# Program's end of a transformer block: norm weights load into two ring rows, finished tiles are stored in the last phase, the last group's splits go first, VectorE norms two tiles

## The reference, cut to what matters

```python
def peer_ffn(x, wq, k1, k2, u, v):
    ...
    def expert_block(args):
        xb, eb, gb = args
        h = jnp.einsum('td,ted->te', xb, u[eb])
        a = jax.nn.gelu(h, approximate=False) * gb
        return jnp.einsum('te,ted->td', a, v[eb])
...
ffn = peer_ffn(h, peer_wq[l], peer_k1[l], peer_k2[l], peer_u[l], peer_v[l])
h = layer_norm(DEEPNORM_ALPHA * h + ffn, ln2_g[l], ln2_b[l])   # (x - mean) * rstd * g + b, over 1024 features
```

## Time and profile before

| what | value |
|---|---|
| median of 3 runs | 3171.38 us (3163.99 to 3172.98) |
| the profiled execution, its own time | 3172.34 us |
| its span, first to last instruction | 3170.7 us |
| VectorE busy, whole span | 2329.7 us (73%) |
| TensorE busy, whole span | 2656.3 us (84%) |
| GpSimd busy, whole span | 1602.5 us (51%) |
| mean granted TensorE clock | 0.925 of full speed |

### The profile page before, as it was taken

How to read it: one execution, slowest core, us unless ns; L and a number is a source line. 1 busy time by engine, 2 the same in 40 slices (tenths; PEclk the granted TensorE clock), 3 DMA queues, 4 the chain that set the end, 5 groups by cost and what they waited for, 6 DMA issues and landing times.

```text
span 3170.7 us, 40717 instructions
## 1 busy us (share of the span) xinstructions
PE 2656.3 (84%) x14888; PEld 2069.8 (65%) x14888; DVE 2329.7 (73%) x4931; ACT 1052.5 (33%) x1647; POOL 1602.5 (51%) x1190
## 2 busy tenths in 40 slices
PE   7997688889996565654667999999999999998886
PEld 6886577777775455642445767676767666776775
DVE  4511566665999799974767778777777887779999
ACT  4311333332554577751112222322222222222222
POOL 0001001112887455536666665766665776756674
PEclk9988799999998788876888999999999999999998
DMA  4222312222111599989999999999999999998994
GB/s 136 93 87 76 129 43 84 84 81 85 51 51 32 183 314 316 308 264 378 379 389 387 384 388 348 397 381 381 388 384 341 407 408 407 406 376 312 338 342 175
DMA packets 309791, 833.42 MB, mean 263 GB/s; under 512 B 26112, under 2 KB 114624, under 8 KB 309600
## 3 DMA queue, kind: packets, MB, share of 16 engines
q0 software_dynamic: 150864, 548.60, 45.3%
q1 hardware_dynamic: 158736, 282.31, 25.5%
HBM read 771.93 MB, written 58.88 MB: 262 GB/s over the span
## 4 chain that ended last, share of the span: by engine, by line
DVE 15%; DMA 13%; PE 10%; POOL 10%; issue 6%; ACT 0%; POOLq 0%; DVEq 0%
DMA e_u_row<-in_u,ids 12%; POOL hold L1904 7%; DVE e_u_row L2123 5%; POOL e_u_row L1895 3%; DVE e_y L2113 3%; PE psum L1965 2%; PE psum L1944 2%; PE psum L1946 1%; PE psum L1945 1%; DVE e_ul L2079 1%; PE psum L1966 1%; PE psum L1967 1%; DVE e_vl L2083 1%; DVE e_al L2100 1%; DVE hold L2132 1%
## 5 line engine op out<-in xcount | busy, mean ns | idle before, releaser
L2123 DVE CUSTOM_DVE_ANT_0 e_u_row<-e_u_row,hold 128x1024 f32<-128x1024 f32 x384 | 468.4, 1225 | 267.4 <-DMA e_u_row<-in_u,ids 248.4
L1895 POOL DMA_INDIRECT e_u_row<-in_u,ids x384 | 483.8, 1260 | 358.1 <-DVE ids L2123 235.3
L1965 PE MATMUL psum<-e_vh,e_ah 128*128 128x512 f32 x1024 | 429.4, 419 | 141.1 <-DVE e_y L2113 101.5
L1904 POOL DMA_INDIRECT hold<-in_v,ids x384 | 431.6, 1124 | 142.1 <-issue 113.0
L1966 PE MATMUL psum<-e_vl,e_ah 128*128 128x512 f32 x1024 | 416.4, 407 | 0.0
L1967 PE MATMUL psum<-e_vh,e_al 128*128 128x512 f32 x1024 | 413.7, 404 | 0.0
L1965 PEld LDWEIGHTS psum<-e_vh,e_ah 128*128 128x128 f32 x1024 | 202.1, 197 | 252.7 <-DVE e_y L2113 138.0
L1944 PE MATMUL psum<-x1d,e_uh 128*128 128x512 f32 x864 | 341.3, 395 | 0.0
L2113 DVE TENSOR_TENSOR e_y<-e_y,psum 128x512 f32<-128x512 f32 x504 | 324.2, 680 | 19.5 <-PE psum L1967 15.1
L1945 PE MATMUL psum<-x1d,e_uh 128*128 128x512 f32 x864 | 337.3, 390 | 0.0
L1946 PE MATMUL psum<-x1d,e_ul 128*128 128x512 f32 x864 | 336.3, 389 | 0.0
(11 more groups left out here) (399 smaller groups left out, 5663.4 us busy)
## 6 DMA issues: line engine op xcount, KB each, us to landing
e_vr<-in_v SPq DMA_DIRECT2D x128, 512.0 KB
e_ur<-in_uT SPq DMA_DIRECT2D x108, 512.0 KB
s_G<-g_tile SPq DMA_DIRECT2D x8, 4096.0 KB, 26.5
e_g<-s_G SPq DMA_DIRECT2D x64, 512.0 KB
ids<-in_w_ch SPq DMA_DIRECT2D x17, 512.0 KB, 4.0
s_ch<-p_out POOLq DMA_DIRECT2D x16, 512.0 KB
hold<-in_wq SPq DMA_DIRECT2D x16, 512.0 KB, 8.9
hold<-in_v,ids POOLq DMA_INDIRECT x476, 6.7
```

What stands on the lines that cost most here:

```text
L1895: pool.indirect_dma_start(out=u_ring[n % U_RING][:], out_offset=None, in_=io["u"], in_offset=bass.IndirectOffsetOnAxis(ap=id_u[:, s, k:k + ...
L1904: pool.indirect_dma_start(out=v_ring[m % V_RING], out_offset=None, in_=io["v"], in_offset=bass.IndirectOffsetOnAxis(ap=id_v[:, t:t + 1], a ...
L1965: nc.tensor.matmul(acc, ah[s][j][:, r], vh[s][j][:, c], start=(j == 0), stop=False)
L2123: nc.vector.tensor_tensor_reduce(row, row, xs[:, s, :], 1.0, 0.0, ALU.mult, ALU.add, hs[:, s, k:k + 1]).then_inc(dotted, 1)
```

## The change

Four parts. (1) The gain and bias are loaded by SP at group 54 into two rows of the ring, which shrinks from 11 to 9 rows. (2) Tiles 0 to 2 get their gain on DVE at the start of groups 56, 57 and 59 (`SCALED`), their bias on POOL after `gather_last(46)`, `(58)` and `(81)` (`SHIFTED`), and their store from SP at the start of groups 60, 61 and 63 (`SENT`). (3) The last group is written out apart, in another order: both v splits and both a splits earlier, the last row sums at its end. (4) Tiles 6 and 7 no longer take shift, ACT, gain and POOL's bias, but two DVE steps: (x - mean) x gain, and that x rstd + bias.

```diff
-        lng, lnb = (ur[j].rearrange("p k e -> p (k e)") for j in range(2))
-        ln_in = 16 * (NG + 1)
+        ln_in = [sem(f"f_ln_in{j}") for j in range(2)]
...
-        sum_ring = u_ring[1:] + v_ring
+        sum_ring = u_ring[1:] + v_ring[:V_RING - 2]
+        lng, lnb = v_ring[V_RING - 2:]
...
+        SCALED = tuple(PHASE[NS - 1] + n for n in (3, 4, 6))
+        SHIFTED = tuple((g + 1 - PHASE[NS - 1]) * P // (NG - PHASE[NS - 1]) for g in SCALED)
+        SENT = tuple(g + 4 for g in SCALED)
...
+                def send(t):
+                    if t < NT - 2:
+                        sp.wait_ge(done, t + 1)
+                    else:
+                        sp.wait_ge(done_last, t - NT + 3)
+                    sp.dma_start(out[0, t * P:(t + 1) * P, :], rows_of(t)).then_inc(stored, 16)
...
+                    if g == PHASE[NS - 1] + 1:
+                        sp.wait_ge(weighted, STEPS)
+                        for row, src, landed in zip((lng, lnb), ("ln2_g", "ln2_b"), ln_in):
+                            sp.dma_start(row, io[src].partition_broadcast(P)).then_inc(landed, 16)
+                    if g in SENT:
+                        send(SENT.index(g))
                     load_gates(g)
...
-                for j, src in enumerate(("ln2_g", "ln2_b")):
-                    sp.wait_ge(u_lo[j], NG - SHORT)
-                    sp.dma_start(ur[j].rearrange("p k e -> p (k e)"), io[src].partition_broadcast(P)).then_inc(u_in[j], 16)
-                for t in range(NT):
-                    sp.wait_ge(done, t + 1)
-                    sp.dma_start(out[0, t * P:(t + 1) * P, :], rows_of(t)).then_inc(stored, 16)
+                for t in range(NS - 1, NT):
+                    send(t)
...
+                def offset(t):
+                    if t == 0:
+                        pool.wait_ge(ln_in[1], 16)
+                    pool.wait_ge(nrm_g, t + 1)
+                    nc.gpsimd.tensor_tensor(rows_of(t), rows_of(t), lnb, ALU.add).then_inc(done, 1)
+
                 for n in range(P):
                     gather_last(n)
-                for t in range(NT):
-                    if t == 0:
-                        pool.wait_ge(u_in[1], ln_in)
-                    pool.wait_ge(nrm_g, t + 1)
-                    nc.gpsimd.tensor_tensor(rows_of(t), rows_of(t), lnb, ALU.add).then_inc(done, 1)
+                    if n in SHIFTED:
+                        offset(SHIFTED.index(n))
+                for t in range(NS - 1, NT - 2):
+                    offset(t)
...
                     if t + 1 < NT:
                         root_of(t + 1)
-                    normalize(t)
+                    if t < NT - 2:
+                        normalize(t)
...
+                def centre_last(t):
+                    dve.wait_ge(aggr, t + 1)
+                    nc.vector.scalar_tensor_tensor(rows_of(t), rows_of(t), mv[:, t, 0:1], lng,
+                                                   ALU.subtract, ALU.mult).then_inc(centred_last, 1)
+
+                def scale_last(t):
+                    dve.wait_ge(rooted, t + 1)
+                    nc.vector.reciprocal(rstd[:, t:t + 1], root[:, t:t + 1]).then_inc(inverted, 1)
+                    dve.wait_ge(inverted, t + 1)
+                    dve.wait_ge(centred_last, t - NT + 3)
+                    dve.wait_ge(ln_in[1], 16)
+                    nc.vector.scalar_tensor_tensor(rows_of(t), rows_of(t), rstd[:, t:t + 1], lnb,
+                                                   ALU.mult, ALU.add).then_inc(done_last, 1)
...
+                    if g in SCALED:
+                        weight(SCALED.index(g))
+                    if g == NG - 1:
+                        break
                     dot_rows(g, 0)
...
+                dot_rows(NG - 1, 0)
+                dot_rows(NG - 1, 1)
+                weigh(NG - 1, 0)
+                split_a(NG - 1, 0)
+                split_v(NG - 1, 0)
+                dot_rows(NG - 1, 2)
+                weigh(NG - 1, 1)
+                split_a(NG - 1, 1)
+                gather(NG - 2, 0, 2)
+                dot_rows(NG - 1, 3)
+                gather(NG - 2, 2, 4)
+                split_v(NG - 1, 1)
+                dot_rows(NG - 1, 4)
+                gather(NG - 2, 4, 6)
+                dot_rows(NG - 1, 5)
+                gather(NG - 2, 6, Q)
+                dot_rows(NG - 1, 6)
+                dot_rows(NG - 1, 7)
                 dve.wait_ge(summed, P)
...
-                for t in range(NS - 1):
-                    weight(t)
-                for t in range(NS - 1, NT + 2):
-                    if t < NT:
-                        if t >= NS:
-                            gather(NG - 1, 2 * (t - NS), 2 * (t - NS) + 2)
-                        statistics(t)
-                    if NS <= t <= NT:
+                for t in range(NS - 1, NT):
+                    if t >= NS:
+                        gather(NG - 1, 2 * (t - NS), 2 * (t - NS) + 2)
+                    statistics(t)
+                    if NS <= t < NT - 1:
                         shift_of(t - 1)
                     if t >= NS + 1:
                         weight(t - 2)
+                    if t == NT - 2:
+                        centre_last(t)
+                scale_last(NT - 2)
+                centre_last(NT - 1)
+                scale_last(NT - 1)
```

More of the change, by code:

```diff
@@ L1815, in experts @@
         v_landed = [sem(f"v_rows_landed{n}") for n in range(V_RING)]
-        s_landed = [sem(f"last_row_landed{n}") for n in range(U_RING - 1 + V_RING)]
+        s_landed = [sem(f"last_row_landed{n}") for n in range(U_RING - 3 + V_RING)]
         dotted = sem("u_row_dotted")
@@ L1822, in experts @@
         stored = sem("f_stored")
+        centred_last, done_last = sem("f_centred_last"), sem("f_done_last")
         stat, aggr, rooted, inverted, shifted, nrm, nrm_g, done = (
@@ L2163, in weight @@
                     dve.wait_ge(nrm, t + 1)
-                    dve.wait_ge(u_in[0], ln_in)
+                    dve.wait_ge(ln_in[0], 16)
                     nc.vector.tensor_tensor(rows_of(t), rows_of(t), lng, ALU.mult).then_inc(nrm_g, 1)
+                def centre_last(t):
[10 more added lines that the diff above has]
+                                                   ALU.mult, ALU.add).then_inc(done_last, 1)
                 nc.vector.memset(column[:], 0.0).then_inc(cleared, 1)
```

## The result

| what | before | after |
|---|---|---|
| median of 20 runs | 3169.37 us | 3180.04 us (3174.82 to 3190.49) |
| ratio after / before | | 1.0035, 95% interval 1.0026 to 1.0044 |
| the profiled execution, its own time | 3172.34 us | 3181.38 us |
| its span | 3170.7 us | 3179.7 us |

The change makes the kernel slower by 10.7 us by the medians, 0.35% by the ratio. The median lies inside the range that was given (3166 to 3182), but the forecast of no change, with 0.87, did not come in: the ratio of 1.0035 lies past the 0.3% bound on the slower side, which had 0.09, though its interval reaches down to 1.0026.

A forecast was written before the change was run, and what follows sets the result against it. The prediction took DVE to bound the last phase. Its terms, -6.0 + 3.4 + 2.55 + 3.7 = +3.65, say +3.7 us on 3171.4, gave a median of 3175 us, range 3166 to 3182, forecast as no change.

The forecast's parts named there:

- The bound: Group 54 to the end of the last group: DVE alone sets the pace, busy 233.85 of 234 us.
- The end behind S: From the last group's end on DVE to the last bias or DVE step: 31.13 us falls to 25.15, -6.0.
- The three gains: Gains of tiles 0 to 2, moved into groups 56, 57 and 59, cost DVE the same time there: +3.4 us.
- POOL's biases: Three biases in the loop: POOL waits until the PSUM additions, DVE loses 1.25 us each, +3.7; bounds 0 and 7.0.
- rival B: POOL gets in at the next boundary each time, DVE loses 2.34 us: +7.0 for the biases, 3178.5 us; chance 0.28.
- the place of 3092.30: Where DVE sums a slot 2 row and begins 7.67 us of instructions with two SBUF inputs; POOL's bias was expected then.
- SP: Loads at group 54, stores at 60, 61 and 63, ahead of the gates: cost nothing; 7.7 us if cover were gone.
- The last group's order: Last group: DVE idles 0.75, 1.1 and 0.7 us before the a splits and a v split, +2.55; bounds 1.5 and 2.6.
- The ring of nine: Ring of fetched rows shrinking from 11 to 9: nine steps give 19.7 us against a fetch's 9.0, so no cost.
- D: Rival: POOL gets in only at the third pair of additions, the ring runs dry: +13.6, 3185 us; chance 0.08.
- C: Rival: the costs in the loop don't come and the real saving of 2.6 us stays: 3169 us; chance 0.12.
- the likeliest case: Over the whole kernel, the sum of all terms, +3.65 us, giving 3175 us; chance 0.52.

The follow-up runs named there:

- late_stores: Changed kernel with the stores of tiles 0 to 2 moved back behind the last group; ratio to the kernel before 1.0025, last stretch 306.2 us.
- extras_behind: Changed kernel with the gain and bias loads and three stores issued behind the second v slab instead of ahead of the gates; ratio 1.0031, last stretch 302.7 us.
- old_last_group: Changed kernel with the old order of the last group; ratio to the kernel before 1.0035, last stretch 306.1 us.
- bias_with_psum: Changed kernel with POOL's biases of tiles 0 to 2 waiting to begin with DVE's additions from PSUM; ratio 1.0022, last stretch 304.1 us.
- two_norms_alone: Kernel before with only the two DVE steps for tiles 6 and 7 (part 4); ratio 0.9995, last stretch 293.0 us.
- three_norms: Kernel before with the two DVE steps for tiles 5, 6 and 7; ratio 1.0001, last stretch 292.0 us.
- gain_as_stt: Kernel before with the gains of tiles 1 and 2 done by scalar_tensor_tensor instead of tensor_tensor; single run, last stretch 295.6 us.
- new_order_alone: Kernel before with only the new order of the last group; ratio 1.0015, last stretch 300.9 us.
- new_order_ring_9: Kernel before with the new order of the last group and a ring of 9 rows instead of 11; ratio 1.0024, last stretch 300.7 us.
- bias_in_row_sums: Changed kernel with POOL's biases of tiles 0 to 2 asked for right behind the last v split of groups 56, 57 and 59; single run, last stretch 317.1 us.

## Why the prediction was off, point by point

**The bound.** Right. DVE sets the pace, and every part of the 12.7 us is a length or an idle time of DVE. (the earlier trace rows start at group 55, not 54; group 54 of the kernel before is the same, 26.14 us busy of 26.14.)

**The end behind S: -6.0.** Right, -6.3. The blocked `scale_last(6)` came as said: 3.50 us from 3169.62 to 3173.12 against 3.64.

**The three gains: +3.4.** Right.

**POOL's biases: +3.7.** This step failed: +6.5, near rival B's 7.0. The step took POOL to wait "until the additions from PSUM", by the row of the three gains in the kernel before, which was called the nearest. POOL got in at the next boundary every time: in groups 56, 57 and 59 of the changed kernel, late_stores, extras_behind and old_last_group, twelve instructions of 3.38 to 3.42 us. (The twelve are one course: POOL's start lies 0.22 to 0.26 us ahead of the boundary in each. In the changed kernel it came to the bias 2.8 to 3.9 us after DVE had reached the place of 3092.30 that the step names, not at it.) What the step took for its price, 1.25, is the price when the bias is made to start with the additions (bias_with_psum), so the size was right for a course that it didn't take. The Trainium skill ("SBUF — State Buffer", Who interferes with whom) has it that whoever issues first has the shared port for its whole instruction. The loop agrees with it: read to the letter it gave 7.0, and 6.5 were measured. Not every row of this case does: in the kernel before, two_norms_alone, three_norms and gain_as_stt POOL asked 0.9 us ahead of a boundary and had to let one more DVE instruction pass. With the new last group, same instructions and same distance, it got in. What decides there stays open.

**SP: 0.** This step failed: +4.0. It weighed 0.5 MB at the whole rate of the DMA engines (1.5 us at 340 GB/s) and against the fetches' slack. But the gates behind it have a slack of their own, 10.4 to 10.9 us, and a transfer of half a megabyte on this queue landed 6.3 to 9.7 us after issue by itself, and 11.0 to 12.4 with another right ahead. The bound given with the step, 7.7 in all if the cover were gone, would have held it. extras_behind shows the cause: with the same bytes behind the slabs, nothing waits for gates. The prediction had named this as its sign of being wrong (idle time on DVE in groups 54 to 62, gates late behind the new stores), and it came.

**The last group's order: +2.55.** The waits were the right ones, the size was not: +5.0. The two waits of 0.7 came as said. The middle one, for the slab's high part, was put at 1.1 with bounds that allowed no more; it is 0.9 to 1.7 in five kernels and 2.2 to 3.2 in three (the whole change, late_stores, bias_with_psum). By itself the order costs 3.1 to 3.3 us (new_order_alone, new_order_ring_9); the other 1.7 of the 5.0 are this wait. The slab took 7.7 us to land in the changed kernel, issued at 3123.43. The ring is not the reason, and the third store at most for a small part (new_order_ring_9 1.3, late_stores 2.7). The reason for the spread is not settled. That the new order is worth its 2.5 us by TensorE's earlier start was also too kind: 2.0 measured (30.75 - 28.78).

**The ring of nine: 0.** Right.

**Rivals.** B was right on its part. D did not come; bias_in_row_sums shows it with POOL held up for 13 us; in bias_with_psum 5.2 us of it did no harm. C did not come. Three terms were too small at once (biases by 2.8 us, SP by 4.0, the last group by 2.45), no single rival covered that, and the likeliest case came out 9 us short on a stretch of 300. That the median still fell into the range is in part luck: the three runs behind the forecast had a median of 3171.4 us, twenty have 3169.4, and the medians differ by 10.7 us where the last stretch of the profiled executions differs by 12.7. With 12.7 on 3171.4 it would have been 3184, outside.

## What to carry to other kernels

Moving work from a program's end into its last stage gains nothing when the same engine is full in that stage: the three gains cost 3.4 us in the loop and had cost 3.4 behind it. It gains only where an instruction or a wait disappears, as POOL's last bias does here. A transfer added to a queue must be weighed against the slack of what stands behind it in that same queue, and at that queue's own landing times, which the trace gives, not at the engines' whole rate. GpSimd's addition of 2.34 us on SBUF beside a full VectorE cost VectorE nearly the whole operation, 2.17 us; started together with additions that read PSUM, it cost 1.25.

## What the runs showed of the hardware that was not expected

- A VectorE instruction over 128 x 1024 elements on two SBUF inputs, in front of which GpSimd has got in, takes 3.36 to 3.42 us instead of 1.22 to 1.28, and counts as busy: groups 56 and 57 show 29.44 of 29.44 and 29.70 of 29.81 us busy while 2.17 us of each are lost.
- Who gets in at a boundary can differ between two kernels with the same instructions at the same distances: behind the last group POOL's first bias, asked for 0.9 us ahead, took 3.18 us with the new last group (the third gain 3.36) and 4.36 to 4.38 with the old one (the third gain 1.21 to 1.24).
- TensorE's granted clock was at half (0.50, the 1.2 GHz level) for a while in the changed kernel's last group: from 3137.88 on a matmul's step was 0.43 us, and from about 3140.7 again 0.23. TensorE had stood without work for 2.21 us ahead of it; in the kernel before, for 3.90 us.

```profile
3137.29 0.80 PE L1984 MATMUL psum<-e_vh,e_ah 128*128 128x512 f32 x1 [2.21 <-DVE e_y L2133]
3137.88 0.63 PE L1985 MATMUL psum<-e_vl,e_ah 128*128 128x512 f32 x1
3138.31 0.63 PE L1986 MATMUL psum<-e_vh,e_al 128*128 128x512 f32 x1
...
3140.70 0.40 PE L1986 MATMUL psum<-e_vh,e_al 128*128 128x512 f32 x1
3140.93 0.39 PE L1984 MATMUL psum<-e_vh,e_ah 128*128 128x512 f32 x1
```
